# Start of a one-core decoder layer: order of the first loads, x turned by k-tile, two chunks interleaved

## The chip, the cores and the metric

The kernel runs on one core of a Trainium2 chip. The metric is the device time of one execution in microseconds; several executions are timed and their median is given. One further execution is profiled, and all rows of the trace below are from that one.

## What is computed

One layer of a decoder with parallel head groups, on 256 prompt tokens and 8 x 8 sample tokens (320 in all), all in float32:

```python
h = rmsnorm(x, g_mix_pre)                 # x: 320 tokens x 2048
p = h @ w_in                              # 2048 x 4352, columns: pool, conv (3 parts), u, v
ya = pool_mixer(p[pool], state_pool, pool_w, pool_scale)      # windows 2, 4, 8, 16
yb = short_conv_mixer(p[conv parts], state_conv, conv_w)
yc = sgu_mixer(p[u], p[v], sgu_norm, sgu_w, sgu_b)            # u * (tril(W) v + b)
x = x + rmsnorm(concat(ya, yb, yc) @ w_out, g_mix_post)
f = conv_ffn(rmsnorm(x, g_ffn_pre), state_ffn, ffn_up, ffn_conv_w, ffn_conv_b, ffn_down)
x = x + rmsnorm(f, g_ffn_post)            # and the new states
```

## The kernel before

Activations are held transposed: a k-tile is 128 features by 320 tokens, and the model width is 16 k-tiles. A product with a weight matrix is made one chunk of 128 output columns at a time. A chunk is 16 k-tiles, and for each k-tile three matmuls (`passes`, L474 to L485): high part by high part, high by low part of the weights, low part of the activations by high. Chunks go in pairs; chunk (q, e) is half e of pair q, accumulates in PSUM bank `mm[e]` and uses half e of `w_hi` and `w_lo`. The first six chunks, pairs 0 to 2, are the columns of u, the next six those of v.

Weights come from DRAM by SP's DMA queue (`load`, L374), 1 MB a chunk in runs of 512 bytes, into one of four places in `raw`. ScalarE copies them, rounded, into `w_hi` in two halves (`split_hi`, L813), and VectorE puts the rest into `w_lo` (`split_lo`, L1093). Counters order this: `landed[e]`, `w_hi_done`, `w_lo_done` (four counts a pair of each), `used` (a chunk's matmuls done) and `drained[e]`. SP's loads have no bound of their own but `w_hi_done`, and its DMAs are issued in program order.

At the start x comes in token order into `x_tok`, in four pieces of 512 columns, each by two DMAs (prompt, sample). TensorE turns it by transposes against an identity matrix (`turn_x`, L538), four k-tiles at a time and three token tiles each, into PSUM banks `tb[1]` to `tb[5]`; ScalarE and VectorE take turns in copying the results into `xT` (`copy_x`). ScalarE then scales and rounds each k-tile of `xT` into `a_hi` (L851), and VectorE makes `a_lo`, the rest (L1151). Chunk (0,0) is computed beside that, with its passes waiting for each k-tile.

After chunk (0,0) TensorE turns the small inputs (`small_inputs`, L562: gains, histories, the gating weights), for which it waits until all of them have landed; VectorE copies the results out of PSUM (L1156 to L1162, `hists_done`), then come chunk (0,1) and the pairs 1 and 2.

The norm's scale is not needed for u and v until late: GpSimd squares and sums the k-tiles of `xT` (`add_square`, L1581), the first eight as x arrives, then, after `hists_done`, a mask on the gating weights (L1598) and the other eight. TensorE reads the sum (`token_sums(0)`, L524) after the sixth chunk, behind a small matmul (`corners`, L589).

Of the kernel before, what the change touches and what calls it, by code (L numbers as in the profile page):

```python
# [31 lines left out]
def hybrid_layer(nc, x_prompt, x_sample, state_pool, state_conv, state_ffn, g_mix_pre, g_mix_post,  # L32
# [155 lines left out]

    with ExitStack() as ctx:
# [13 lines left out]
        x_in = [sem(f"x_in{i}") for i in range(KD // 4)]  # L203
# [87 lines left out]
        X_UNITS = 3 * (KD // 4)  # L291
# [3 lines left out]
        def x_units(k4, e):  # L295

            return [u for u in range(3 * k4, 3 * k4 + 3) if u % 2 == e] if k4 < KD // 4 else []

        def wait_x(engine, k4):

            for e in range(2):
                engine.wait_ge(x_copied[e], (3 * k4 + 4 - e) // 2)

        def x_unit(u):

            k4, i = u // 3, u % 3
            t0, nt = TT[i]
            return (xT[:, :].rearrange("p (k t) -> p k t", t=T)[:, 4 * k4:4 * k4 + 4, t0:t0 + nt],
                    tb[1 + u % 5][:, 0:4 * nt].rearrange("p (k t) -> p k t", k=4))
# [25 lines left out]
        def stage_vecs(q):  # L335
            rows = 0
            for v in (g_mix_pre, g_mix_post, g_ffn_pre, g_ffn_post, conv_w, sgu_norm, pool_scale):
                n = v.shape[-1] // P * (3 if v is conv_w else 1)
                src = v[0].rearrange("i (j c) -> (i j) c", c=P) if v is conv_w else \
# [26 lines left out]
        def _(sp):  # L366
# [20 lines left out]
            load(0, 0, wcols(win_v, U0))  # L387
# [13 lines left out]
            for e in range(2):  # L401
                load(1, e, wcols(win_v, U0 + 2 + e))
# [71 lines left out]
        def _(pe):  # L474
# [63 lines left out]
            def turn_x(k4):  # L538

                pe.wait_ge(x_in[k4], 32)  # L540
                for i in range(3):
                    u = 3 * k4 + i
                    if u >= 5:
                        pe.wait_ge(x_copied[(u - 5) % 2], (u - 5) // 2 + 1)
                    nt = TT[i][1]
                    for k in range(4):
                        b = 4 * k4 + k
                        last = pe.transpose(tb[1 + u % 5][:, k * nt:(k + 1) * nt],
                                            x_tok[0:nt, i, b * P:(b + 1) * P], ident[0:nt, 0:nt])
                    last.then_inc(x_turned, 1)  # L550


            pe.wait_ge(gain_in, 16)
            pe.transpose(tb[0][:, 0:KD], vec_raw[0:KD, 0, :], ident[0:KD, 0:KD]).then_inc(vecs_t, 1)
# [3 lines left out]
            turn_x(0)  # L558
            chunk(0, 0, a_hi, a_lo, order, lambda n: (a_hi_done, n + 1), lambda n: (a_lo_done, n + 1),
                  {n: [lambda k4=k4: turn_x(k4)] for k4, n in ((1, 0), (2, 1), (3, 5))})  # L560

            def small_inputs():  # L562
# [6 lines left out]
                for e in range(2):  # L569
                    pe.wait_ge(x_copied[e], X_UNITS // 2)  # L570
# [20 lines left out]

            small_inputs()
            chunk(0, 1, a_hi, a_lo, order, hurry=True)
# [1122 lines left out]
```

## Time and profile before

| | |
|---|---|
| median of 3 runs | 1370.25 us (1367.58 to 1371.25) |
| the profiled execution | 1367.87 us, its span 1366.1 us |
| TensorE busy | 1335.0 us, 98% |
| VectorE, ScalarE, GpSimd busy | 762.2, 504.9, 116.4 us |
| DMA over the span | 199.55 MB, 146 GB/s |
| mean granted TensorE clock | 0.993 |

The span is the time from the first to the last recorded instruction; about 1.8 us of the execution lie outside it. Busy time of TensorE counts overlapping pieces once; a matmul of 320 columns is recorded at 0.31 us, and the next one starts 0.15 us after it when nothing is waited for. The interval from one start to the next is what a matmul costs.

### The profile page before, as it was taken

What the parts mean: (1) busy time and instruction counts of PE and PEld (TensorE: products, weight loads), DVE (VectorE), ACT (ScalarE), POOL (GpSimd) and SP (SyncE); (2) the same over time, 40 slices, a digit from 0 to 9 for tenths busy, and PEclk for the clock granted to TensorE, in tenths of its full rate; (3) what the DMA queues carried; (4) which work ended last, traced back from release to release, by engine and by line L of the source; (5) the groups of instructions that cost most, each with busy time, mean ns of one, the idle gap of its engine ahead of it and who ended that gap; (6) DMA issues with size and microseconds to landing.
All of it is one profiled execution on the core that took longest, in us unless ns stands there. A gap on an engine that the chain in (4) does not pass through costs nothing.

```text
span 1366.1 us, 24821 instructions
## 1 busy us (share of the span) xinstructions
PE 1335.0 (98%) x9003; PEld 1319.6 (97%) x9003; DVE 762.2 (56%) x1170; ACT 504.9 (37%) x730; POOL 116.4 (9%) x225
## 2 busy tenths in 40 slices
PE   6999999999989999999999999999999999999997
PEld 5999999999978999999999999999999999999995
DVE  6447755553358655544555654455555445656445
ACT  4333422334345333333333333333333333333653
POOL 4542000000025000000000000000000000000001
PEclk9999999999989999999999999999999999999999
DMA  8555355555543555456555545655544565554453
GB/s 232 160 143 154 99 154 154 151 133 149 157 124 95 152 154 145 117 148 181 147 154 152 145 124 150 169 150 154 154 126 134 148 175 154 154 149 129 118 155 100
DMA packets 379007, 199.55 MB, mean 146 GB/s; under 512 B 3924, under 2 KB 374592, under 8 KB 378968
## 3 DMA queue, kind: packets, MB, share of 16 engines
q1 hardware_dynamic: 378896, 198.83, 53.0%
q8 instruction: 19, 0.31, 0.1%
q0 software_dynamic: 80, 0.31, 0.1%
q14 instruction: 12, 0.10, 0.0%
HBM read 195.68 MB, written 3.56 MB: 146 GB/s over the span
## 4 chain that ended last, share of the span: by engine, by line
PE 94%; DVE 2%; SPq 2%; POOL 1%; DMA 0%; issue 0%; ACT 0%; DVEq 0%; ACTq 0%
PE mm L481 30%; PE mm L485 30%; PE mm L482 30%; POOL xT L1652 1%; SPq L341 1%; PE tb L732 1%; DVE y_tok L1536 1%; DMA sgu_bias<-in_sgu_b_dram 0%; DVE sq L1375 0%; DVE w_lo L1102 0%; PE tb L524 0%; SPq L355 0%; PE tb L481 0%; PE tb L482 0%; PE tb L485 0%
## 5 line engine op out<-in xcount | busy, mean ns | idle before, releaser
L481 PE MATMUL mm<-a_hi,w_hi 128*128 128x320 f32 x1888 | 586.9, 311 | 0.0
L485 PE MATMUL mm<-a_lo,w_hi 128*128 128x320 f32 x1888 | 584.2, 309 | 1.8 <-DVE a_lo L1151 1.8
L482 PE MATMUL mm<-a_hi,w_lo 128*128 128x320 f32 x1888 | 583.7, 309 | 0.0
L824 ACT ACTIVATE w_hi<-raw 128x1024 fp32r (+3 forms) x396 | 364.9, 970 | 448.8 <-PE mm L485 435.5
L1102 DVE TENSOR_TENSOR w_lo<-raw,w_hi 128x1024 fp32r<-128x1024 f32 (+1 forms) x396 | 434.7, 1139 | 130.7 <-ACT w_hi L824 130.6
L485 PEld LDWEIGHTS mm<-a_lo,w_hi 128*128 128x128 f32 x1888 | 354.6, 188 | 2.7 <-DVE a_lo L1151 2.5
L481 PEld LDWEIGHTS mm<-a_hi,w_hi 128*128 128x128 f32 x1888 | 354.8, 188 | 1.2
L482 PEld LDWEIGHTS mm<-a_hi,w_lo 128*128 128x128 f32 x1888 | 354.9, 188 | 0.3
L485 PE MATMUL mm<-m_lo,w_hi 128*128 128x320 f32 x916 | 283.1, 309 | 0.0
L481 PE MATMUL mm<-h_hi,w_hi 128*128 128x320 f32 x660 | 205.7, 312 | 0.0
L482 PE MATMUL mm<-h_hi,w_lo 128*128 128x320 f32 x660 | 203.9, 309 | 0.0
L485 PEld LDWEIGHTS mm<-m_lo,w_hi 128*128 128x128 f32 x916 | 171.9, 188 | 0.0
L482 PEld LDWEIGHTS mm<-h_hi,w_lo 128*128 128x128 f32 x660 | 124.0, 188 | 0.0
L481 PEld LDWEIGHTS mm<-h_hi,w_hi 128*128 128x128 f32 x660 | 123.9, 188 | 0.0
L1435 DVE TENSOR_TENSOR f<-mm,f 128x320 f32 (+1 forms) x60 | 29.5, 492 | 130.7 <-PE mm L485 130.7
L970 ACT ACTIVATE h_hi<-val 128x320 f32 (+1 forms) x44 | 20.8, 472 | 191.7 <-DVE val L1422 191.7
L1666 POOL COPY ffn_tail_p<-zf 128x2 f32 x44 | 15.0, 340 | 804.4 <-DVE zf L1402 804.4
L481 PE MATMUL mm<-m_hi,w_hi 128*128 128x320 f32 x256 | 79.2, 309 | 0.0
L482 PE MATMUL mm<-m_hi,w_lo 128*128 128x320 f32 x256 | 79.1, 309 | 0.0
L1419 DVE TENSOR_TENSOR val<-mm,r_v 128x320 f32<-128x320 f32 x42 | 20.7, 492 | 84.1 <-PE mm L485 84.1
L1398 DVE COPY zf<-ffn_hist 128x16 f32 (+1 forms) x44 | 7.8, 176 | 96.1 <-PE mm L485 94.4
L482 PEld LDWEIGHTS mm<-m_hi,w_lo 128*128 128x128 f32 x256 | 48.1, 188 | 0.0
(241 smaller groups left out, 833.9 us busy)
## 6 DMA issues: line engine op xcount, KB each, us to landing
raw<-in_ffn_up_dram SPq DMA_DIRECT2D x88, 1024.0 KB, 5.7
raw<-in_ffn_down_dram SPq DMA_DIRECT2D x60, 704.0 KB, 4.8
raw<-in_w_in_dram SPq DMA_DIRECT2D x34, 1024.0 KB, 5.6
raw<-in_w_out_dram SPq DMA_DIRECT2D x16, 1024.0 KB, 6.0
x_tok<-in_x_prompt_dram SPq DMA_DIRECT2D x4, 512.0 KB, 7.5
raw<-in_ffn_down_dram SPq DMA_DIRECT2D x2, 1024.0 KB, 5.6
out_dram<-y_tok SPq DMA_DIRECT2D x8, 256.0 KB
raw<-in_ffn_down_dram SPq DMA_DIRECT2D x1, 768.0 KB, 4.3
```

Of the source, the lines that this page charges most:

```text
L341: yield q.dma_start(vec_raw[rows:rows + n, 0, :], src)
L481: pe.matmul(out, w_hi[:, s], hi, start=start, stop=False)
L482: pe.matmul(out, w_lo[:, s], hi, start=False, stop=False)
L485: return pe.matmul(out, w_hi[:, s], tile(lo, k), start=False, stop=stop)
L732: last = pe.transpose(bank[0:nt, k * P:(k + 1) * P], src[:, o:o + nt], ident[:, :])
L824: act.activation(w_hi[:, d:d + half], src, ACT.Copy).then_inc(w_hi_done, 1)
L970: act.activation(h_tile(i, 0, T), val[:, :], ACT.Copy).then_inc(h_hi_done, 1)
L1102: dve.tensor_tensor(w_lo[:, d], src, w_hi[:, d].bitcast(F32), ALU.subtract).then_inc(w_lo_done, 1)
L1419: dve.tensor_tensor(val[:, :], val_mm[:, 0:T], r_v[:, :], ALU.mult).then_inc(drained[1], 1)
L1435: dve.tensor_tensor(tile(f, m), mm[e][:, 0:T], tile(f, m), ALU.add).then_inc(drained[e], 1)
L1536: dve.scalar_tensor_tensor(out=piece, in0=f_tok[3 * k4 + i][0:nt, :], scalar=cols[0:nt, 2, i:i + 1], in1=piece, op0=ALU.mult, op1=ALU.add) ...
L1666: pool.tensor_copy(ffn_tail_p[:, bass.ds(n * CH, CH)], zf[:, LC - CH:LC])
```

## The change

- SP's first DMAs are in another order. x comes in five parts of 2, 2, 4, 4, 4 k-tiles. The weights of chunk (0,0) come in parts of 4, 4 and 8 k-tiles, those of (0,1) in two of 8, and they stand between the parts of x. The load of chunk (1,0) is issued after a wait on `w_hi_done`, and ahead of the small inputs; that of (1,1) after them. The first gain vector is issued from ScalarE's queue.
- x is turned one k-tile at a time, three transposes into one PSUM bank of six. ScalarE and VectorE make `a_hi` and `a_lo` straight from PSUM, and copy `xT` beside that, ScalarE the even and VectorE the odd k-tiles.
- Chunks (0,0) and (0,1) are interleaved: in step n come the turning of k-tile n + 2, the passes of k-tile n for chunk (0,0), and those of k-tile n - 10 for chunk (0,1).
- The weights of the two are split in the same parts, between the k-tiles: after k = 0, 4, 6, 11 and the last, on ScalarE into `w_hi` and on VectorE into `w_lo`.
- The small inputs are turned after chunk (1,0), and VectorE copies them after it has split the weights of chunk (1,1).
- GpSimd starts its squares when the weights of the first pair are all split and all of x is copied.

```diff
+    X_PARTS = [(0, 2), (2, 2), (4, 4), (8, 4), (12, 4)]
...
+            load_x(0)
+            load_part(0, 0, 4, w_in_part[0])
+            load_x(1)
+            load_x(2)
+            load_part(0, 4, 4, w_in_part[1])
+            load_part(0, 8, 8, landed[0])
+            load_x(3)
+            load_part(1, 0, 8, w_in_part[2])
+            load_x(4)
+            load_part(1, 8, 8, landed[1])
+            sp.wait_ge(w_hi_done, 2)
+            load(1, 0, wcols(win_v, U0 + 2))
             vecs = stage_vecs(sp)
-            next(vecs).then_inc(gain_in, 16)
-            for k4 in range(KD // 4):
-                cs = slice(k4 * 512, (k4 + 1) * 512)
-                sp.dma_start(x_tok[:, 0:2, cs], xp[:, :, cs]).then_inc(x_in[k4], 16)
-                sp.dma_start(x_tok[0:TS, 2, cs],
-                             x_sample.rearrange("b t d -> (b t) d")[:, cs]).then_inc(x_in[k4], 16)
-            load(0, 1, wcols(win_v, U0 + 1))
+            next(vecs)
             for d in vecs:
                 d.then_inc(vecs_in, 16)
             for d in stage(sp):
                 d.then_inc(staged, 16)
-            for e in range(2):
-                load(1, e, wcols(win_v, U0 + 2 + e))
+            sp.wait_ge(w_hi_done, 4)
+            load(1, 1, wcols(win_v, U0 + 3))
...
+            def turn_x(k):
+                n = X_PART[k]
+                if k == X_PARTS[n][0]:
+                    pe.wait_ge(x_in[n], 32)
+                if k >= 6:
+                    pe.wait_ge(*copied(k - 6))
+                for t0, nt in TT:
+                    last = pe.transpose(tb[k % 6][:, t0:t0 + nt], x_tok[0:nt, t0 // P, k * P:(k + 1) * P],
+                                        ident[0:nt, 0:nt])
+                last.then_inc(x_turned, 1)
...
+            AHEAD, LAG = 2, 10
+            for k in range(AHEAD):
+                turn_x(k)
+            pe.wait_ge(vecs_done, 1)
+            for n in range(KD + LAG):
+                k = n
+                if k < KD:
+                    if k + AHEAD < KD:
+                        turn_x(k + AHEAD)
+                    if k == 0:
+                        pe.wait_ge(first_lo, 1)
+                    if k in (4, 8):
+                        pe.wait_ge(w_lo_done, k // 4)
+                    last = passes(mm[0][:, 0:T], 0, k, a_hi, a_lo, k == 0, k == KD - 1,
+                                  (a_hi_done, k + 1), (a_lo_done, k + 1))
+                    if k == KD - 1:
+                        last.then_inc(used, 1)
+                k = n - LAG
+                if k >= 0:
+                    if k in (0, 8):
+                        pe.wait_ge(w_lo_done, 3 + k // 8)
+                    last = passes(mm[1][:, 0:T], 1, k, a_hi, a_lo, k == 0, k == KD - 1)
+                    if k == KD - 1:
+                        last.then_inc(used, 1)
...
+            chunk(1, 0, a_hi, a_lo, order)
             small_inputs()
-            chunk(0, 1, a_hi, a_lo, order, hurry=True)
-            with pe.Fori(1, NSGU // 2) as q:
+            chunk(1, 1, a_hi, a_lo, order)
+            with pe.Fori(2, NSGU // 2) as q:
                 pair(q, a_hi, a_lo, order)
...
+            act.dma_start(vec_raw[0:KD, 0, :], g_mix_pre[0].rearrange("(j c) -> j c", c=P)).then_inc(gain_in, 16)
...
             for k in range(KD):
-                if k % 4 == 1:
-                    copy_x(k // 4 + 1)
-                if k % 4 == 0:
-                    wait_x(act, k // 4)
-                act.activation(tile(a_hi, k), tile(xT, k), ACT.Copy,
+                act.wait_ge(x_turned, k + 1)
+                act.activation(tile(a_hi, k), tb[k % 6][:, 0:T], ACT.Copy,
                                scale=col(V_MIX_PRE + k)).then_inc(a_hi_done, 1)
-            split_hi(0, 1)
+                if k % 2:
+                    act.wait_ge(a_lo_done, k)
+                    act.activation(tile(xT, k - 1), tb[(k - 1) % 6][:, 0:T], ACT.Copy).then_inc(x_copied[0], 1)
+                if k == 0:
+                    split_part(0, 0, 4, w_in_part[0], first_hi)
+                if k == 4:
+                    split_part(0, 4, 4, w_in_part[1], w_hi_done)
+                if k == 6:
+                    split_part(0, 8, 8, landed[0], w_hi_done)
+                if k == 11:
+                    split_part(1, 0, 8, w_in_part[2], w_hi_done)
+            split_part(1, 8, 8, landed[1], w_hi_done)
...
                 dve.wait_ge(a_hi_done, k + 1)
-                dve.scalar_tensor_tensor(out=tile(a_lo, k), in0=tile(xT, k), scalar=col(V_MIX_PRE + k),
+                dve.scalar_tensor_tensor(out=tile(a_lo, k), in0=tb[k % 6][:, 0:T], scalar=col(V_MIX_PRE + k),
                                          in1=tile(a_hi, k).bitcast(F32), op0=ALU.mult,
                                          op1=ALU.subtract).then_inc(a_lo_done, 1)
-            split_lo(0, 1)
+                if k % 2:
+                    dve.tensor_copy(tile(xT, k), tb[k % 6][:, 0:T]).then_inc(x_copied[1], 1)
...
+            for e in range(2):
+                split_lo(1, e)
             dve.wait_ge(hists_t, 1)
...
-            for e in range(2):
-                split_lo(1, e)
...
+            pool.wait_ge(w_lo_done, 4)
+            for e in range(2):
+                pool.wait_ge(x_copied[e], KD // 2)
             for k in range(KD):
-                if k % 4 == 0:
-                    wait_x(pool, k // 4)
```

## Rows read from the trace of the kernel before

**Rows 1.** The page, engines: busy us (share of the span) xinstructions.
```profile
PE 1335.0 (98%) x9003; PEld 1319.6 (97%) x9003; DVE 762.2 (56%) x1170; ACT 504.9 (37%) x730; POOL 116.4 (9%) x225
```
**Rows 2.** The chain that ended last: shares, then one piece (start us, us).
```profile
PE 94%; DVE 2%; SPq 2%; POOL 1%; DMA 0%; issue 0%; ACT 0%; DVEq 0%; ACTq 0%
...
70.97 0.76 PE tb L524 x6
```
**Rows 3.** Timeline of PE (start us, us, what, count [idle before]), and a window with PEclk.
```profile
9.20 2.58 PE L548 MATMUL tb<-ident,x_tok 128*128 128x128 f32 x12 [1.70 <-DMA x_tok<-in_x_sample_dram]
...
15.39 0.47 PE L482 MATMUL mm<-a_hi,w_lo 128*128 128x320 f32 x1
15.65 0.47 PE L485 MATMUL mm<-a_lo,w_hi 128*128 128x320 f32 x1
...
20.41 1.42 PE L548 MATMUL tb<-ident,x_tok 128*128 128x128 f32 x12
...
31.68 0.63 PE L573 MATMUL tb<-ident,pool_raw 120*128 120x120 f32 x4 [1.82 <-DMA sgu_bias<-in_sgu_b_dram]
...
39.03 0.31 PE L482 MATMUL mm<-a_hi,w_lo 128*128 128x320 f32 x1
39.18 0.31 PE L485 MATMUL mm<-a_lo,w_hi 128*128 128x320 f32 x1
...
32.00:35.70 3.70, 3.70 (x19) 0.56 1.17 297
```
**Rows 4.** Timeline of ACT and DVE; then durations of two lines, min/median/max ns.
```profile
6.47 2.00 ACT L824 ACTIVATE w_hi<-raw 128x1024 fp32r<-128x1024 f32 x2 [4.38 <-DMA raw<-in_w_in_dram]
...
36.55 2.01 ACT L824 ACTIVATE w_hi<-raw 128x1024 fp32r<-128x1024 f32 x2 [6.46 <-DMA raw<-in_w_in_dram]
42.61 0.44 ACT L858 ACTIVATE f<-mm 128x320 f32<-128x320 f32 x1 [4.04 <-PE mm L485]
...
34.91 0.42 DVE L1156 COPY vec<-tb 128x252 f32<-128x252 f32 x1 [3.49 <-PE tb L582]
...
37.50 0.35 DVE L1162 COPY ffn_hist<-tb 128x192 f32<-128x192 f32 x1
37.76 3.02 DVE L1102 TENSOR_TENSOR w_lo<-raw,w_hi 128x1024 fp32r<-128x1024 f32 x2
...
L1151 DVE SCALAR_TENSOR_TENSOR a_lo<-xT,vec,a_hi x16: 535/1002/1160, 13.0 to 28.6; 128x320 fp32r<-128x320 f32 x16
...
L1220 DVE SCALAR_TENSOR_TENSOR m_lo<-tb,vec,m_hi x4: 546/550/551, 136.0 to 164.3; 128x320 fp32r<-128x320 f32 x4
```
**Rows 5.** Timeline of POOL: first square, eighth sum, mask, last sum.
```profile
12.29 0.72 POOL L1583 TENSOR_TENSOR acc<-xT 128x320 f32<-128x320 f32 x1 [8.41 <-ACT xT L842]
...
25.95 1.00 POOL L1586 TENSOR_TENSOR acc<-acc,sq 128x320 f32<-128x320 f32 x1
38.01 1.70 POOL L1598 TENSOR_SCALAR_AFFINE_SELECT ws<-ws 128x768 f32<-128x768 f32 x1 [11.06 <-DVE ffn_hist L1162]
...
57.29 0.88 POOL L1586 TENSOR_TENSOR acc<-acc,sq 128x320 f32<-128x320 f32 x1
```
**Rows 6.** Timeline of SP's queue; then landing times of the loads into raw.
```profile
8.41 0.61 SPq L385 DMA_DIRECT2D raw<-in_w_in_dram  x1
9.06 7.64 SPq L341 DMA_DIRECT2D vec_raw<-in_g_mix_post_dram  x1
...
26.58 4.85 SPq L385 DMA_DIRECT2D raw<-in_w_in_dram  x2
...
27.35 4.08 SPq L385 DMA_DIRECT2D raw<-in_w_in_dram  x1
...
DMA to landing us min/median/max: 5.6/8.1/12.2
```
**Rows 7.** Windows from the span's start: length, PEclk, DMA share, GB/s.
```profile
0.00:16.70 16.70, 1.00 0.93 249
0.00:31.43 31.43, 1.00 0.85 225
```

More of the change, by code:

```diff
@@ L187, in hybrid_layer @@
     ffn_out = sb("ffn_out", [P, 7, P], where="m_hi", plus=NG * HW * 4)
+    X_PARTS = [(0, 2), (2, 2), (4, 4), (8, 4), (12, 4)]
+    X_PART = [n for n, (k0, nk) in enumerate(X_PARTS) for _ in range(nk)]
     with ExitStack() as ctx:
@@ L202, in hybrid_layer @@
         drained = [sem(f"drained{i}") for i in range(2)]
-        x_in = [sem(f"x_in{i}") for i in range(KD // 4)]
+        x_in = [sem(f"x_in{i}") for i in range(len(X_PARTS))]
+        w_in_part = [sem(f"w_in_part{i}") for i in range(3)]
+        first_hi = sem("first_hi")
+        first_lo = sem("first_lo")
         gain_in = sem("gain_in")
@@ L289, in tile, with copied @@
             return t[:, k * T:(k + n) * T] if type(k) is int else t[:, bass.ds(k * T, n * T)]
-        X_UNITS = 3 * (KD // 4)
         MERGED = (4, 9)
         EARLY = 2
-        def x_units(k4, e):
-            return [u for u in range(3 * k4, 3 * k4 + 3) if u % 2 == e] if k4 < KD // 4 else []
-        def wait_x(engine, k4):
-            for e in range(2):
[L302 to L309, printed above, removed]
+        def copied(k):
+            return x_copied[k % 2], k // 2 + 1
         def h_tile(i, lo, hi):
@@ L338, in stage_vecs @@
                 n = v.shape[-1] // P * (3 if v is conv_w else 1)
+                if v is g_mix_pre:
+                    yield None
+                    rows += n
+                    continue
                 src = v[0].rearrange("i (j c) -> (i j) c", c=P) if v is conv_w else \
@@ L385, in load, with load_x, load_part @@
                 sp.dma_start(dst.rearrange("p (k c) -> p k c", c=width), src).then_inc(landed[e], 16)
-            load(0, 0, wcols(win_v, U0))
             xp = x_prompt[0].rearrange("(t p) d -> p t d", p=P)
-            vecs = stage_vecs(sp)
-            next(vecs).then_inc(gain_in, 16)
-            for k4 in range(KD // 4):
-                cs = slice(k4 * 512, (k4 + 1) * 512)
-                sp.dma_start(x_tok[:, 0:2, cs], xp[:, :, cs]).then_inc(x_in[k4], 16)
-                sp.dma_start(x_tok[0:TS, 2, cs],
-                             x_sample.rearrange("b t d -> (b t) d")[:, cs]).then_inc(x_in[k4], 16)
-            load(0, 1, wcols(win_v, U0 + 1))
+            def load_x(n):
+                k0, nk = X_PARTS[n]
+                cs = slice(k0 * P, (k0 + nk) * P)
+                sp.dma_start(x_tok[:, 0:2, cs], xp[:, :, cs]).then_inc(x_in[n], 16)
+                sp.dma_start(x_tok[0:TS, 2, cs],
+                             x_sample.rearrange("b t d -> (b t) d")[:, cs]).then_inc(x_in[n], 16)
+            def load_part(e, k0, nk, sem):
+                o = (e * KD + k0) * P
+                sp.dma_start(raw[:, o:o + nk * P].rearrange("p (k c) -> p k c", c=P),
+                             wcols(win_v, U0 + e)[:, k0:k0 + nk]).then_inc(sem, 16)
+            load_x(0)
[10 more added lines that the diff above has]
+            load(1, 0, wcols(win_v, U0 + 2))
+            vecs = stage_vecs(sp)
+            next(vecs)
             for d in vecs:
@@ L536, in _ @@
             pe.wait_ge(consts, 1)
[L538 to L550, printed above, removed]
@@ L553, in _ @@
-            pe.wait_ge(gain_in, 16)
-            pe.transpose(tb[0][:, 0:KD], vec_raw[0:KD, 0, :], ident[0:KD, 0:KD]).then_inc(vecs_t, 1)
-            order = range(KD)
-            turn_x(0)
-            chunk(0, 0, a_hi, a_lo, order, lambda n: (a_hi_done, n + 1), lambda n: (a_lo_done, n + 1),
-                  {n: [lambda k4=k4: turn_x(k4)] for k4, n in ((1, 0), (2, 1), (3, 5))})
+            def turn_x(k):
[8 more added lines that the diff above has]
+                last.then_inc(x_turned, 1)
@@ new lines, in _ @@
+            order = range(KD)
+            pe.wait_ge(gain_in, 16)
+            pe.transpose(mm[1][:, 0:KD], vec_raw[0:KD, 0, :], ident[0:KD, 0:KD]).then_inc(vecs_t, 1)
+            AHEAD, LAG = 2, 10
[22 more added lines that the diff above has]
+                        last.then_inc(used, 1)
```

40 lines of the change are left out of this document (20 added, 20 removed).

## The prediction

> **What bounds the kernel now.** I read the page's engine table first: TensorE is busy 98% of the span, the next engine, VectorE, 56% [rows 1]. The chain that ended last puts 94% on TensorE and 2% on the SP queue [rows 2], so the only place where loads cost time is the start. From about 36 us on TensorE runs one matmul after the other: starts 0.15 us apart (39.03 to 39.18), 48 of them to a chunk, 7.05 us a chunk, with ScalarE draining the second chunk at 42.61 [rows 3, 4]. Two chunks are 14.1 us of that work, so 28.5 us of the first 42.6 are something else. The reader is to see four things in the timeline there: TensorE starts turning x only at 9.20, behind 1 MB of weights; early matmuls start 0.26 us apart (15.39, 15.65), which is the 1.2 GHz level, against 0.15 at 2.4 GHz; it waits 1.82 us for the last small input at 31.68; and it is granted only 0.56 of its clock from 32 to 35.7 [rows 3, 6]. After that nothing stops it until the sum of squares is read at 70.97 [rows 2], and I take that matmul as the landmark: all behind it is unchanged and follows on it, so what it moves by is what the kernel moves by. It needs two chains: TensorE's own six chunks, and GpSimd's squares, which now end at 58.2, 12.8 us early [rows 5].
>
> **Loads.** The x pieces and the first weights are cut and mixed; the sum is the same until both first chunks are in, 2.62 MB of x and 2.10 MB of weights. Before, 1.05 MB had landed at 6.47 (ScalarE's wait) and the second block, 4.73 MB in, at 20.6 (8.41 plus the longest landing, 12.2) [rows 4, 6]. That is 0.26 MB per us. The new last x part ends at 4.19 MB, so it lands at 6.47 + 3.14/0.26 = 18.5, the first x part (0.33 MB) at about 4 (two microseconds after issue, an estimate; x at 4 or at 6 changes nothing below). x begins earlier and does not end earlier. The gain vector goes to ScalarE's queue and is off the path: it is wanted at 4, and even the 5.6 us of the shortest landing in the list [rows 6] would delay only k-tiles that wait for x afterwards. SP's two new waits, on the second and fourth high weight part, hold every later load behind them; the parts land at 11.5 and 20.5 by the same rate and are split 1 to 5 us later, before SP is free again at 16.7 and 30.2, as worked out below, so they cost nothing. ScalarE's wait for the part of chunk (0,1), landing at 16.0, holds up k-tile 12, which is not there before 18.5.
>
> **First two chunks.** TensorE is in order and turns k-tile 12 before the passes of k-tile 10, so it cannot go beyond k-tile 9 before 18.5, whatever VectorE does. Behind that lie 12 transposes at 0.12 (1.42 us for 12 [rows 3]) and 6 + 16 passes of 3 matmuls, 66 x 0.147 = 9.7: 11.1 us, end 29.6. TensorE has waited for x shortly before, so I add low clock: 3.7 us at 0.56 [rows 3] cost some 1.6, and all 66 at 0.26 would cost 7.5. I take 1.5: both chunks end at 31, between 29.6 and 38. VectorE and ScalarE are not the bound here: 16 splits at 0.55 (a split read from PSUM took 0.55, and one beside GpSimd's squares up to 1.16 [rows 4]), 8 copies at 0.5 and 3.5 us of weight splits are 16.3 us from about 5.5; even at 1.0 a split the last four need less than TensorE's 1.23 us a k-tile. Copies of xT lie beside that. The Trainium skill ("TensorE: Matmul & The Clock Gate", Part 1) says that throttled is the default state and activity releases it; the trace agrees (0.26 us apart at the start, 0.15 later). By that rule the waits for x keep the clock low, which by the rows above would put the end at 31.2 and not 29.6; it speaks for the late side.
>
> **Third chunk and small inputs.** Chunk (1,0) is 7.05: 38. Its weights wait until chunk 0 releases the buffers 4.8 us before chunk 1 ends; drain 0.4, first half by ScalarE 1.0, two halves by VectorE 2.4 to 3.0 make 3.8 to 4.4, so nothing is lost. The small inputs are 20 transposes; the last 17 took 3.2 us at mostly low clock before, 31.68 to VectorE's start at 34.91 [rows 3, 4], and 20 at 0.12 are 2.4 at the high one, which I take: TensorE is ready for chunk (1,1) at 40.5. The 1.8 us wait for them is gone.
>
> **The fourth chunk's load.** This is the term that decides. SP's issues are held back when too much is outstanding: the first small input was issued at 9.06 and went through after 7.64, at 16.7, when 249 GB/s x 16.7 = 4.16 of 4.84 MB had moved, 0.68 MB left; the load issued at 27.35 went through at 31.43, when 7.07 of 7.72 MB had moved, 0.64 left [rows 6, 7]. Now load (1,0), 1.05 MB, stands ahead of the small inputs, and at the full-queue rate of 0.27 MB per us they begin 4.0 us later, 20.7 for 16.7. SP then issues the same 19 DMAs, one each 0.5 us, and load (1,1) at 26.58 + 4.0 = 30.6. The load that stood in that place, with another behind it as now, was first touched at 36.55, 10.0 us after its issue [rows 4, 6]. So load (1,1) lands at 40.5. ScalarE takes 1.05 for the first half, VectorE 2.35 to 3.02 for both (3.02 beside GpSimd): chunk (1,1) can start at 44.3, and TensorE waits 3.8 us. Counting bytes alone, all up to that load were through at 33.5 before, so the slowest of the rings cost the rest; if that is not repeated it lands at 37.5 to 38.5. Both ends are kept.
>
> **Squares.** GpSimd now starts when the fourth part of the low weights is there, about 27, and its first eight squares took 14.7 (12.29 to 26.95) [rows 5]: 42 to 45 with the weight splits beside. The second eight wait for the small inputs' copies. These stand behind the split of chunk (1,1) on VectorE, 44.3, and took 2.94 (34.91 to 37.85): 47.2. From 37.85 to the end of the squares at 58.2 was 20.3 with the mask in it [rows 4, 5]: 67.5. TensorE's own chain: 44.3 + 7.05 + 1.6 to 2.0 of low clock after the wait + 14.1 = 67.1 to 67.5. Both meet at 67.5, and the 12.8 us of slack of the squares is used up. Weights of later chunks are a chunk ahead and come through.
>
> **Sum.** The landmark goes from 71.0 to 67.5: 3.5 us less. The profiled execution took 1367.87 (span 1366.1 and 1.8 around it), so 1364.4 by its own time. That is 2.4 below the median of the runs, 1370.25, so 1366.8 in those terms. A difference of 0.3%, 4.1 us, is what a measurement can tell from none.
>
> **Rivals.**
> A, the forecast: the fourth chunk's load decides, gain 2.6 to 4.6. Chance 0.50.
> B: the load comes by bytes, at 38.5 or before. For it: landings are 5.6 us when the queue is short, against it the 10.0 of the same place. Chunk (1,1) can start at 42.1, copies end at 45.0, squares at 65.3: gain 5.7. With the load no bound at all the small inputs are, at 40.5: squares at 63.7, then low clock 1.6 after TensorE's wait of 2 us, 65.3, gain 5.7. So the squares cap what a quicker start may bring. About 1364.5, chance 0.22.
> C: the small inputs come 1 to 3 us later still, or the first two chunks end at 35 to 37 (three separate waits for x at low clock), or GpSimd's first eight run into the second. Gain 0.5 to 2.6, about 1368.7, chance 0.22.
> D, the other side: the clock stays at the 1.2 GHz level through the first chunks, as each new wait (k-tiles 4, 8, 12) comes before it rises. 66 matmuls at 0.26 and 12 transposes at 0.21 from 18.5 end at 38.2; small inputs end at 48.8, squares at 72.0: 1 us slower. Low clock in chunk (1,0) too, 48 at 0.26 for 7.05, makes it 77.5, 6.5 us slower, 1376.8. It turns to a loss when the two chunks end after 37. Against it: 2.4 GHz was reached by 19 before, in spite of the 1.70 us wait, and a TensorE at the low clock is late enough to have few waits left. Chance 0.06.
>
> **Numbers.** Faster by over 0.3%: all but a little of B and the upper quarter of A, 0.20 + 0.14 and 0.03 for scatter: 0.37. Slower by over 0.3%: most of D, 0.04. Within: 0.59. The range goes from B less a microsecond (1363.0) to C's far end (1370.0), which leaves out D and the tails; A's own is 1365.6 to 1367.7.
>
> **What would show it.** Right: the last x transposes after 18; TensorE idle for 3 to 4 us before chunk (1,1) with the low weights as releaser; SP's first small input going through near 20.7; the first token sum at 67 to 68 with the squares ending just there; splits of x at 0.55. Wrong, if load (1,1) lands before 38, if TensorE does not wait before chunk (1,1), or if it waits for GpSimd by more than 2 us; if the landmark moves and the total does not, the step that all behind it follows fails.

## The result and the profile after

| | before | changed |
|---|---|---|
| median of 20 runs | 1370.22 us (1367.49 to 1371.69) | 1371.46 us (1369.13 to 1378.31) |
| ratio to before | | 1.0025, 95% interval 1.0016 to 1.0034 |
| profiled execution, span | 1367.87, 1366.1 us | 1373.18, 1371.4 us |
| first token sum starts (timeline of TensorE) | 70.90 us | 74.65 us |

The change makes the kernel slower by a quarter of a per cent. The forecast was 1366.8, faster by 3.5 us. The medians are 1.2 us apart and the means, 1369.8 and 1373.0, 3.2, because the changed kernel scatters: 11 of the 20 executions of the changed kernel lie between 1369.1 and 1371.8, 7 between 1374.0 and 1378.3, while those of before keep within 4.2 us. So what it lost differs from one execution to the next, and the profiled one, at 1373.18, is none of the 11: all rows of the changed kernel below tell how that one execution lost its 5.3 us of span.

I look first for the landmark, the first token sum. [rows 2] put it at 70.97 by the chain; by the timeline, which I use from here on for every run, it starts at 70.90 in the kernel before:

```profile
70.90 0.83 PE L524 MATMUL tb<-ones,acc 128*128 128x1 f32 x6
```

Timeline of TensorE in the changed kernel (start, length, instruction, what it waited for):

```profile
5.21 1.90 PE L561 MATMUL tb<-ident,x_tok 128*128 128x128 f32 x6 [2.02 <-DMA x_tok<-in_x_sample_dram]
7.32 0.96 PE L561 MATMUL tb<-ident,x_tok 128*128 128x128 f32 x3 [0.21 <-DMA x_tok<-in_x_sample_dram]
...
10.99 0.93 PE L561 MATMUL tb<-ident,x_tok 128*128 128x128 f32 x3
11.85 0.63 PE L496 MATMUL mm<-a_hi,w_hi 128*128 128x320 f32 x1
12.28 0.47 PE L497 MATMUL mm<-a_hi,w_lo 128*128 128x320 f32 x1
12.55 0.47 PE L500 MATMUL mm<-a_lo,w_hi 128*128 128x320 f32 x1
12.81 0.93 PE L561 MATMUL tb<-ident,x_tok 128*128 128x128 f32 x3
...
25.55 0.93 PE L561 MATMUL tb<-ident,x_tok 128*128 128x128 f32 x3
...
34.93 0.31 PE L497 MATMUL mm<-a_hi,w_lo 128*128 128x320 f32 x1
35.07 0.31 PE L500 MATMUL mm<-a_lo,w_hi 128*128 128x320 f32 x1
...
48.85 0.40 PE L599 MATMUL tb<-ident,vec_raw 92*128 92x92 f32 x3
...
51.09 0.41 PE L496 MATMUL mm<-a_hi,w_hi 128*128 128x320 f32 x1
...
74.65 0.92 PE L539 MATMUL tb<-ones,acc 128*128 128x1 f32 x6 [1.94 <-POOL acc L1631]
```

TensorE has x four microseconds sooner than in [rows 3] (5.21 against 9.20), and but for 0.21 us at 7.32 it does not wait for x again. One k-tile's turning and one k-tile's passes go round in 1.82 us, 10.99 to 12.81, and again 14.63, 16.45 and so on to 25.55. In that round the three transposes take 0.86 us, the first matmul behind them 0.43, and then matmuls start 0.27 us apart, which is the 1.2 GHz level; 0.15 us, the 2.4 GHz level, is seen from 34.7 on. The last line is the landmark, and it waits for GpSimd.

Windows of the changed kernel (length, PE busy, PEclk, DMA share, GB/s):

```profile
5.00:34.00 29.00, 28.35 (x93) 1.00 0.93 239
70.00:75.00 5.00, 3.06 (x22) 1.00 0.52 137
75.00:80.00 5.00, 5.00 (x26) 0.66 0.81 211
```

TensorE is busy in 28.35 of the 29 us from 5 to 34 and yet at half its speed. The clock column shows 1.00 there, but the trace holds no record of the clock before 34.3 us, so a first rise has to be read from the distance of two starts. From 75 to 80, behind the wait for GpSimd, the column does show a fall to 0.66; before, this stretch was at the full clock.

Timeline of the changed kernel on ScalarE, VectorE, GpSimd and the SP queue, in the same columns (for SP the second number is how long the issue took, or a run of alike issues from the first to the last):

```profile
42.01 0.44 ACT L898 ACTIVATE f<-mm 128x320 f32<-128x320 f32 x1 [2.51 <-PE mm L500]
42.40 2.01 ACT L858 ACTIVATE w_hi<-raw 128x1024 fp32r<-128x1024 f32 x2
...
53.79 0.35 DVE L1209 COPY ffn_hist<-tb 128x192 f32<-128x192 f32 x1
...
37.93 0.72 POOL L1628 TENSOR_TENSOR acc<-xT 128x320 f32<-128x320 f32 x1 [34.05 <-DVE w_lo L1182]
...
53.59 0.88 POOL L1631 TENSOR_TENSOR acc<-acc,sq 128x320 f32<-128x320 f32 x1
54.54 1.73 POOL L1644 TENSOR_SCALAR_AFFINE_SELECT ws<-ws 128x768 f32<-128x768 f32 x1
...
73.74 0.86 POOL L1631 TENSOR_TENSOR acc<-acc,sq 128x320 f32<-128x320 f32 x1
...
17.52 4.29 SPq L338 DMA_DIRECT2D vec_raw<-in_g_mix_post_dram  x1
...
31.14 0.55 SPq L354 DMA_DIRECT2D sgu_bias<-in_sgu_b_dram  x1
36.61 50.84 SPq L382 DMA_DIRECT2D raw<-in_w_in_dram  x8
```

The view of one line in the changed kernel, VectorE's low parts of x: least, median and longest duration in ns, first start and last end in us, and what VectorE waited for ahead of them (us, times):

```profile
L1186 DVE SCALAR_TENSOR_TENSOR a_lo<-tb,vec,a_hi x16: 544/550/552, 6.9 to 35.3; 128x320 fp32r<-128x320 f32 x16
its engine sat idle before it (us, times) until:
  ACT a_hi L880: 16.3, 12
```

Both first chunks are done at 42.0, as late as the second one was before (42.6 in [rows 4]), though the small inputs are not among them any more. VectorE makes each low part in 0.55 us and sits idle for 16.3 us between them, so it isn't the pace. The copies of the small inputs end at 54.14 (before 37.85), GpSimd's squares at 74.6, 20.5 after that, and TensorE, which would have been there at 72.7, waits 1.94 us. The landmark is 3.75 us late (1.8 of TensorE's own work and 1.94 of waiting), and the low clock behind it makes up the rest of the 5.3 us of the span.

### The profile page after: what moved, and what is told of

Its sections match the earlier page's. It is cut to its first block, busy times and chain, and to the rows that moved or that the text cites. A ratio compares the mean times of both kernels' runs of the same rounds, so it can differ in the third digit from the quotient of the medians.

```text
span 1371.4 us, 24821 instructions
## 1 busy us (share of the span) xinstructions
PE 1346.2 (98%) x9003; PEld 1325.6 (97%) x9003; DVE 760.3 (55%) x1173; ACT 505.4 (37%) x733; POOL 118.2 (9%) x225
## 4 chain that ended last, share of the span: by engine, by line
PE 92%; POOL 4%; DVE 2%; issue 0%; ACT 0%; DMA 0%; SPq 0%; DVEq 0%; ACTq 0%
PE mm L496 30%; PE mm L497 29%; PE mm L500 29%; POOL xT L1698 1%; POOL acc L1631 1%; POOL sq L1628 1%; PE tb L561 1%; PE tb L765 1%; DVE y_tok L1581 0%; DMA x_tok<-in_x_sample_dram 0%; DVE sq L1420 0%; DVE w_lo L1142 0%; PE tb L539 0%; PE tb L496 0%; PE tb L497 0%
## 5 line engine op out<-in xcount | busy, mean ns | idle before, releaser
L858 ACT ACTIVATE w_hi<-raw 128x1024 fp32r (+3 forms) x392 | 360.9, 969 | 437.7 <-PE mm L500 435.3
L1464 DVE TENSOR_TENSOR val<-mm,r_v 128x320 f32<-128x320 f32 x42 | 20.7, 492 | 84.1 <-PE mm L500 84.1
L496 PEld LDWEIGHTS mm<-m_hi,w_hi 128*128 128x128 f32 x256 | 48.1, 188 | 0.0
```

Of the source, the lines that this page charges most:

```text
L496: pe.matmul(out, w_hi[:, s], hi, start=start, stop=False)
L858: act.activation(w_hi[:, d:d + half], src, ACT.Copy).then_inc(w_hi_done, 1)
L1464: dve.tensor_tensor(val[:, :], val_mm[:, 0:T], r_v[:, :], ALU.mult).then_inc(drained[1], 1)
```

## The experiments

Rows one to four, five to eight and nine to twelve of the table share a chip each, and the ratio is to the executions of the kernel before on that chip (medians 1369.87, 1369.30 and 1369.70). Each run has 11 or 12 executions, the last two have five. "Both end" is where ScalarE starts to drain the second chunk; the wait in the last column is for GpSimd's squares.

| run | median us | ratio, 95% interval | both end | first token sum, its wait |
|---|---|---|---|---|
| squares early | 1370.94 | 1.0007, 0.9995 to 1.0018 | 41.96 | 74.32, 1.66 |
| and mask last | 1371.70 | 1.0013, 1.0003 to 1.0023 | 39.57 | 70.69, none |
| no interleave | 1372.86 | 1.0022, 1.0011 to 1.0032 | 41.98 | 74.35, 1.67 |
| 14 extra matmuls | 1369.65 | 0.9993, 0.9980 to 1.0005 | 36.94 | 69.55, 1.91 |
| 14 extra, squares early, mask last | 1367.03 | 0.9983, 0.9974 to 0.9992 | 37.89 | 68.52, none |
| bursts of four | 1368.04 | 0.9991, 0.9979 to 1.0002 | 34.49 | 67.83, 1.63 |
| 6 extra, no interleave, squares early, mask last | 1370.48 | 0.9999, 0.9982 to 1.0017 | 42.38 | 73.00, none |
| kernel before with 14 extra | 1366.97 | 0.9983, 0.9973 to 0.9993 | 40.49 | 68.79, none |
| bursts by token tile | 1366.19 | 0.9983, 0.9973 to 0.9993 | 32.01 | 67.60, 1.61 |
| that, 14 extra, squares early, mask last | 1366.66 | 0.9980, 0.9971 to 0.9989 | 33.57 | 66.52, none |
| that, load (1,1) earlier | 1362.40 | 0.9952, 0.9939 to 0.9966 | 32.28 | 63.39, none |
| the same without extra matmuls | 1361.73 | 0.9947, 0.9934 to 0.9961 | 34.53 | 65.53, none |

The last two columns are of one profiled execution each, which need not be near the median.

**Squares early.** One part undone:

```diff
-            pool.wait_ge(w_lo_done, 4)
-            for e in range(2):
-                pool.wait_ge(x_copied[e], KD // 2)
             for k in range(KD):
+                pool.wait_ge(*copied(k))
                 if k == KD // 2:
```

> The changed kernel with one part undone: GpSimd squares each k-tile as soon as it is copied, as before; the mask still stands in the middle. Theory 1 (the start is paced by TensorE at the 1.2 GHz level; GpSimd's second half is what the first token sum waits for, and it starts at the copies of the small inputs at 54.1): first half done by 45, second half from 54.2, first token sum at 74.3 instead of 74.65, total within 1 us of the changed kernel. Theory 2 (holding the squares back until the weights are split is the loss): token sum at 72.7, total 3.5 us less. The low parts of x read one PSUM and one SBUF operand: if GpSimd's squares slow them they take up to 1.0 us instead of 0.55.

The token sum moved by 0.33 us, as theory 1 had it: GpSimd's mask starts at 54.24, 0.3 earlier than with the squares late. Holding back the squares cost those 0.3 us in this trace, since the first half ran 0.3 past the copies; the rest of the wait comes from what the second half hangs on. The median is half a microsecond below the changed kernel's, measured on another chip, and that can't be told from nothing.

**Mask last.** The wait for the small inputs' copies out of the squares:

```diff
-                if k == KD // 2:
-                    pool.wait_ge(hists_done, 1)
-                    pool.affine_select(out=ws[:, :, :], in_=ws[:, :, :], compare_op=ALU.is_ge, fill=0.0,
-                                       base=0, pattern=[[0, NSGU], [1, P]],
-                                       channel_multiplier=-1).then_inc(tril_done, 1)
                 add_square(tile(xT, k), k == 0, k == KD - 1)
+            pool.wait_ge(hists_done, 1)
+            pool.affine_select(out=ws[:, :, :], in_=ws[:, :, :], compare_op=ALU.is_ge, fill=0.0,
+                               base=0, pattern=[[0, NSGU], [1, P]],
+                               channel_multiplier=-1).then_inc(tril_done, 1)
```

> As the run before, and the mask on the gating weights after all sixteen squares instead of between eighth and ninth. Theory 1: nothing of the squares waits for the small inputs any more, they end before 56; TensorE reaches the first token sum at 72.7 and does not wait, and the low clock behind that wait (0.66 in 75 to 80) is gone: 1.9 and 1.6, together 3.5 us less than the changed kernel, about level with the kernel before. Theory 2 gives nothing beyond the run before.

The wait at the token sum is gone, and so is the low clock behind it; the profiled execution took 1369.16, 3.6 less than the one with the squares early. But the median did not fall (1371.70, against 1370.94 for the squares early on the same chip), and the trace shows why one execution says little here: in this one the clock rose at 21 and fell again after a wait. Timeline of TensorE with the mask last:

```profile
20.14 0.47 PE L500 MATMUL mm<-a_lo,w_hi 128*128 128x320 f32 x1
20.40 0.93 PE L561 MATMUL tb<-ident,x_tok 128*128 128x128 f32 x3
21.26 0.41 PE L496 MATMUL mm<-a_hi,w_hi 128*128 128x320 f32 x1
21.51 0.30 PE L497 MATMUL mm<-a_hi,w_lo 128*128 128x320 f32 x1
21.65 0.31 PE L500 MATMUL mm<-a_lo,w_hi 128*128 128x320 f32 x1
...
26.68 0.42 PE L496 MATMUL mm<-a_hi,w_hi 128*128 128x320 f32 x1 [1.54 <-DVE w_lo L1182]
```

The same instructions that stayed at 0.27 us until 34 in the changed kernel's trace are at 0.15 from 21 here, at 0.27 again from 28 to 31. So the cut into single k-tiles does not forbid the high clock; it leaves open when it comes. The expected 3.5 us of median was a miss, and no run shows what the wait at the token sum costs in the median.

**No interleave.**

```diff
-            AHEAD, LAG = 2, 10
+            AHEAD, LAG = 2, 16
```

> The changed kernel without the interleave: chunk (0,1) follows chunk (0,0), 16 k-tiles behind instead of 10. Theory 1, with the transposes as what keeps the clock low: four steps of 0.8 us at the low clock move behind the last transpose and run at 0.147 a matmul; both chunks end 1.1 to 1.5 us earlier than 42.0. If the second chunk's matmuls are what raises the clock, it rises later and both end at 42 to 44. A theory in which x's landing paces the start gives no change before k-tile 10 and an end later by none.

A miss of the 1.1 to 1.5 us: both end at 41.98. The low-clock steps of 1.82 us go on to 33.4, and the clock rises at 34.3, where it did with the interleave. In this trace the second chunk's passes among the first's neither cost nor gain.

**Fourteen extra matmuls.** Float32 matmuls of 128 columns whose results nobody reads, before the first x is turned, to have the clock up:

```diff
             AHEAD, LAG = 2, 10
+            for _ in range(14):
+                pe.matmul(tb[5][:, 0:P], ones[:, :], ident[:, :], start=True, stop=True)
```

> The changed kernel with 14 extra float32 matmuls of 128 columns, whose results nobody reads, on TensorE before the first x k-tile is turned (about 3.2 to 8.5 us, so x is turned some 3 us later than it could be). Theory 1: the clock is at 2.4 GHz from about 7.5 on and the start holds it; steps of a k-tile go from 1.82 to 0.9 us until TensorE waits for x; both chunks end at 30 to 33 instead of 42.0, and then the terms of the prediction that were never reached decide: chunk (1,1) waits for its load until 44, token sum at 67 to 69. Rival (work cut this fine does not hold the clock): it falls back to matmuls 0.26 apart, both chunks end at 43 to 45. Rival (loads of x pace the start): both chunks end at 42 or later in spite of a high clock.

Timeline of TensorE with 14 extra matmuls (a float32 matmul of this kind is recorded as two, hence x28):

```profile
3.20 5.75 PE L571 MATMUL tb<-ident,ones 128*128 128x128 f32 x28
8.79 1.73 PE L561 MATMUL tb<-ident,x_tok 128*128 128x128 f32 x9
11.31 0.41 PE L496 MATMUL mm<-a_hi,w_hi 128*128 128x320 f32 x1 [0.79 <-DVE w_lo L1184]
...
12.92 0.58 PE L561 MATMUL tb<-ident,x_tok 128*128 128x128 f32 x3
...
13.98 0.58 PE L561 MATMUL tb<-ident,x_tok 128*128 128x128 f32 x3
...
24.07 0.42 PE L496 MATMUL mm<-a_hi,w_hi 128*128 128x320 f32 x1 [1.45 <-DVE w_lo L1184]
```

The round of a k-tile falls from 1.82 to 1.06 us and stays there until 22, so the loads of x were not the pace, and the finely cut work holds a high clock that it has. Both end at 36.94, five microseconds earlier though x is turned 3.6 later; the 30 to 33 expected did not come, because of that start, the 1.45 us wait at k-tile 10 and a fall of the clock behind it (25.1 to 28.6). The load of chunk (1,1) was first touched at 40.20, waited for by ScalarE alone. GpSimd still holds the token sum for 1.91 us.

**Both losses taken away.** The two losses are the low clock of the first chunks and the wait at the token sum. The edits of "squares early", "mask last" and "fourteen extra matmuls" together (these unread matmuls are added work in every run that has them):

> The run with 14 extra float32 matmuls (results unread) and the run with the mask after all squares, together. Theory (low clock through the first chunks, and GpSimd's squares behind the small inputs' copies, are the two losses and add up): TensorE reaches the first token sum at 67.3 as in the run with extra matmuls alone, does not wait there (1.9 there), and the low clock of 70 to 77 behind it is gone: median 1366 to 1367, some 3.5 below the run with extra matmuls alone (1369.65). Rival (the low clock behind the wait has nothing to do with it, or the load of chunk (1,1) takes over): 1369 or more.

1367.03, 2.6 below the extra matmuls alone, but on another chip; by the ratios, 0.9983 and 0.9993, it is 1.4, and their intervals overlap. From 68 to 77 the clock is full, where it was 0.57 from 69 to 77 in the run with extra matmuls alone. So both losses are gone from the trace (token sum at 68.52, expected 67.3), and that they add up in the median is not shown.

**Bursts of four.** x turned four k-tiles at a time, all else as changed:

```diff
-                    if k + AHEAD < KD:
-                        turn_x(k + AHEAD)
+                    for t in {0: (2, 3), 2: (4, 5, 6, 7), 6: (8, 9, 10, 11), 10: (12, 13, 14, 15)}.get(k, ()):
+                        turn_x(t)
```

> The changed kernel with x turned in bursts of four k-tiles (12 transposes, as before), all else as changed. Theory A (turning by single k-tiles costs TensorE time by itself: three transposes and the change to matmuls take 0.86 us at the low clock, 12 in a row 2.5): 0.9 us less for four k-tiles, both chunks end near 38.7 even if the clock does not rise earlier. Theory B (and it is the fine cut that keeps the clock low): in the kernel before, with bursts, it rose near 18.8; here too it is up by 20, k-tile steps go to about 1 us, and both chunks end at 32 to 35. If neither, they end at 41 to 42.

Timeline of TensorE with bursts of four:

```profile
10.89 3.67 PE L561 MATMUL tb<-ident,x_tok 128*128 128x128 f32 x12
14.48 0.63 PE L496 MATMUL mm<-a_hi,w_hi 128*128 128x320 f32 x1
...
22.28 2.31 PE L561 MATMUL tb<-ident,x_tok 128*128 128x128 f32 x12
24.52 0.41 PE L496 MATMUL mm<-a_hi,w_hi 128*128 128x320 f32 x1
```

ScalarE in the same trace:

```profile
34.49 0.44 ACT L898 ACTIVATE f<-mm 128x320 f32<-128x320 f32 x1 [2.51 <-PE mm L500]
40.52 2.01 ACT L858 ACTIVATE w_hi<-raw 128x1024 fp32r<-128x1024 f32 x2 [5.58 <-DMA raw<-in_w_in_dram]
```

Theory B, and not A: 12 transposes take 3.6 us at the low clock (10.89 to 14.48), four times 0.90, so a burst in itself saves nothing on the transposes. But the clock is up by 20.4 and both end at 34.49. One edit of the order on TensorE takes back 7.5 of the first 42 us, and 3.4 us of median against the changed kernel (on another chip; the intervals of the two ratios, to 1.0002 and from 1.0016, do not meet). Now the load of chunk (1,1) holds ScalarE from 34.9 to 40.52.

**Six extra matmuls, no interleave, mask last.** The edits of "both losses taken away" (squares early too), with two numbers changed:

```diff
-            AHEAD, LAG = 2, 10
-            for _ in range(14):
+            AHEAD, LAG = 2, 16
+            for _ in range(6):
```

> A version made from the findings: 6 extra matmuls instead of 14 (so that x is not held back), the second chunk after the first, squares early and the mask last. Theory (a start at the high clock is what counts): k-tile steps of 1.06 us from about 8.5, or from 10 if six are too few to raise it; both chunks end at 32.5 to 34.5, first token sum at 63 to 65.5 unless the load of chunk (1,1) takes over, which landed at 40.2 in the run with 14: then at 67. Median 1364 to 1368. Rival: six are too few, the clock stays low as in the changed kernel, both chunks end at 41 to 42.

In the profiled execution six were too few: 1.82 us a round, both end at 42.38, the rival's case. The 12 executions fall in two clumps, five from 1363.1 to 1366.1 and six from 1372.1 to 1373.4, 7 us apart. The one profiled is of the upper clump and started at the low clock; that the lower ones started at the high clock is likely, but no trace of one is kept. The expected 1364 to 1368 was a miss.

**The kernel before with the extra matmuls.** Nothing of the change is in it:

```diff
+            for _ in range(14):
+                pe.matmul(tb[5][:, 0:P], ones[:, :], ident[:, :], start=True, stop=True)
             pe.wait_ge(gain_in, 16)
```

> The kernel before with the same 14 extra matmuls, where TensorE waits for the first vector and x in any case. Theory (the start of the kernel before is bound by the landing of the small inputs at 31.68, not by TensorE): the clock is high from the first k-tile on and chunk (0,0) may end earlier, but the small inputs are turned at the same time; only the low clock of 32 to 35.7 might change; landmark at 69.5 to 71, median within 1.5 us of the kernel before. Rival (TensorE's low clock bounds that start too): chunk (0,0) and all behind it 2 to 4 us earlier.

Part of it was wrong. The small inputs are turned at 31.10, 0.6 earlier, so their landing does bound that start; but the stretch from 32 to 35.7, at 0.56 in [rows 3], is now at the full clock. Window of that run (length, PE busy, PEclk, DMA share, GB/s):

```profile
32.00:35.70 3.70, 3.70 (x28) 1.00 1.20 290
```

The landmark is at 68.79, 2.1 earlier, and the median 2.3 lower. I had called the start of before not bound by TensorE; the 0.6 us and some 1.6 of low clock were its own. On this one chip two runs can be compared: the kernel before with 14 extra matmuls takes 1366.97, and the changed kernel with them and both fixes of the squares 1367.03. With the clock high from the start in both, the change gains nothing.

**Bursts by token tile.** Inside a burst, the four tiles of tokens 0 to 127 first, then the next four, then the four of 64 samples:

```diff
...
+                for t0, nt in TT:
+                    for k in ks:
+                        ins = pe.transpose(tb[k % 6][:, t0:t0 + nt],
+                                           x_tok[0:nt, t0 // P, k * P:(k + 1) * P], ident[0:nt, 0:nt])
+                        if t0 == TT[-1][0]:
+                            ins.then_inc(x_turned, 1)
...
```

> The changed kernel, x turned in bursts of four k-tiles and inside a burst by token tile (four of 128 tokens, four of 128, four of 64) instead of 128, 128, 64 for each k-tile. Theory (going from a 128-row tile to a 64-row one and back costs by itself; 12 transposes took 3.6 at the low clock in the run with bursts and 2.5 in the kernel before): 12 take 2.5 at the low clock and 1.45 at the high one, both chunks end 2 to 4 us before the 34.5 of that run, unless x's landing takes over. The first token sum does not move below 67, since the load of chunk (1,1) lands at 40 and GpSimd's second half hangs on the small inputs: median 1367 to 1368.5. Rival: 12 still take 3.6; nothing changes.

Timeline of TensorE in that run:

```profile
15.77 1.48 PE L574 MATMUL tb<-ident,x_tok 128*128 128x128 f32 x12 [0.26 <-DMA x_tok<-in_x_sample_dram]
19.93 1.48 PE L574 MATMUL tb<-ident,x_tok 128*128 128x128 f32 x12 [0.73 <-DMA x_tok<-in_x_sample_dram]
...
44.36 0.41 PE L496 MATMUL mm<-a_hi,w_hi 128*128 128x320 f32 x1 [3.21 <-DVE w_lo L1156]
```

ScalarE and the SP queue in the same trace: the load of chunk (1,1) is first touched at 40.86 and was issued at 32.15, the first of nine alike:

```profile
40.86 2.00 ACT L872 ACTIVATE w_hi<-raw 128x1024 fp32r<-128x1024 f32 x2 [8.41 <-DMA raw<-in_w_in_dram]
32.15 52.95 SPq L382 DMA_DIRECT2D raw<-in_w_in_dram  x9
```

12 transposes take 1.48 us for 2.31, with the same clock and the same work, so going between 128-row and 64-row tiles costs by itself. Which PSUM bank they write is not the reason: sorted transposes take 1.42 with four in a row in one bank ([rows 3]) and 1.48 with each in another. Both end at 32.01, and x's landing is now felt: the last part is there at 19.93, after a wait of 0.73. TensorE waits 3.21 us for chunk (1,1), which starts at 44.36; the prediction had 3.8 and 44.3. With 1366.19 it is below the expected 1367 to 1368.5. In this trace the clock was up by 12.6, where it took the bursts of four until 18 to 20; in the last run below, with the same sorted bursts, matmuls start 0.27 apart until 17.7, so the sorting alone does not bring it.

**With extra matmuls, squares early and mask last; then the load moved.** The first of these two runs is the bursts by token tile and the edits of "both losses taken away" together. The second is the first with load (1,1) in front of the small inputs. The last weight part of the first pair gets a semaphore of its own, so that this load need not wait on the fourth high part:

```diff
...
             load(1, 0, wcols(win_v, U0 + 2))
+            load(1, 1, wcols(win_v, U0 + 3))
             vecs = stage_vecs(sp)
...
-            sp.wait_ge(w_hi_done, 4)
-            load(1, 1, wcols(win_v, U0 + 3))
...
```

> That, with the 14 extra matmuls, squares early and the mask last. Theory: the first chunks end at 31 to 33, TensorE waits 2 to 4 us before chunk (1,1) for its load (landed at 40.2 to 40.7 in three runs, split until 44), as the prediction had it; first token sum at 66 to 67, no wait there; median 1365 to 1366.5. Rival (the load is no bound): first token sum at 63 to 64, 1363.

> The run before this one with the load of chunk (1,1) issued ahead of the small inputs instead of behind them. Theory (that load's place in the queue is the next bound): it lands before 30, small inputs land near 39.5, where TensorE wants them; chunk (1,1) starts at 41 to 43 instead of 44 to 45; first token sum at 62.5 to 64.5; 1362 to 1364.5. Rival (small inputs now come later and hold TensorE as much): they land after 43, no gain.

Against the bursts by token tile alone (1366.19, same chip) the first of the two gains nothing, 1366.66, though its wait at the token sum is gone: the extra matmuls hold back x, both end at 33.57 instead of 32.01, and the load of chunk (1,1) is touched at 41.46. Then the load moves: token sum from 66.52 to 63.39, median from 1366.66 to 1362.40. Its place in the queue is worth 4 us once the first chunks are quick. In the second trace TensorE waits 0.3 us for the small inputs at 39.78 and not at all for chunk (1,1).

**Without the extra matmuls.** The run with the load moved, without its 14 unread matmuls:

> The same without the 14 extra matmuls. Theory: x is turned from 5.3 instead of 9, the clock rises near 18 to 20 by itself; both chunks end at 31 to 34, first token sum at 63 to 66; 1363 to 1366. Rival (without the extra matmuls the clock stays low in most executions): both end at 38 to 42, median 1369 or more.

1361.73, ratio 0.9947, below the expected 1363 to 1366: the lowest median of the study, some 7 us below the kernel before (0.0053 of 1369.7), though it can't be told from the run with the extra matmuls (0.9952; the intervals overlap). Five executions, 1361.4 to 1365.6; the profiled one is the slowest of them. With bursts by token tile the extra matmuls are not needed.

## Why the prediction was wrong

**The step that failed** is "first two chunks": both at 31, "between 29.6 and 38". They ended at 42.0. I let TensorE stand at k-tile 9 until x's last part landed at 18.5, and priced only what lies behind it: 12 transposes at 0.12 and 66 matmuls at 0.147, 1.5 us added for the clock. TensorE reached that place at 25.55, 7 us after I had x landed, because the ten rounds before it cost 1.82 us each, a price I never worked out because I had them hidden behind x's landing. From there to the end of both it took another 16.5 us, where I had 11.1 and 1.5 for the clock.

Three terms make the 1.82. The clock: the extra matmuls bring it to 1.06 with nothing else changed. The order of the transposes: 0.86 for three, where the rows that I took the price from [rows 3] are sorted by tile shape; sorted, 12 cost 1.48, unsorted 2.31 at the same clock. And the change from transposes to matmuls: the first matmul behind them costs 0.43 for 0.27 (0.25 for 0.15 at the high clock), once in every round of the fine cut and once in four k-tiles with bursts.

The first term was rival D, to which I gave 0.06 and an end at 38.2. D was right about the clock and wrong about its reason, since it wanted new waits for x. My argument against it, that a TensorE at the low clock has few waits left, was true (0.23 us of waits from 8 to 34) and no argument: the clock stayed low without waits. One of the signs that I had named for being wrong came: TensorE does not wait before chunk (1,1).

**Where the forecast does come true** is the run with bursts by token tile: x's last part at 19.93 (18.5), both chunks at 32.01 (31), chunk (1,1) at 44.36 after 3.21 of waiting (44.3, 3.8), token sum at 67.60 (67.5), median 1366.19 (1366.8; the kernel before is at 1369.70 on that chip). With the order of the transposes that I had priced, the sum was sound; part of that is luck, as the load below shows, and there TensorE waits 1.61 for GpSimd, where I had none.

**When the clock rose.** That activity releases the throttle (the Trainium skill, "TensorE: Matmul & The Clock Gate", Part 1) I weighed only through waits. The traces agree that the clock comes up with work, and they show TensorE busy in 28.35 of 29 us at the low level. It was up by 20.4 with the same transposes in bursts, and at 21 in one execution without. In the other four traces of the fine cut that did not start high it rose at 34.0 to 35.4, with the last transposes of x or behind them. What about a burst raises it, no run here isolates.

**The squares** were right as a chain. Second half ending 20.3 us after the copies (measured 20.5), all slack used up, TensorE waiting: 1.94 us. I had both chains meet without a wait; the low clock behind the wait, priced under B at 1.6, came too. As a start I gave 27, and it was 37.93, again by the first step; the first half then ran until 54.47, 0.3 past the end of the copies at 54.14, so that any later end of it would have cost in full.

**The fourth chunk's load**, which I named as the term that decides, did not in the changed kernel: ScalarE splits it at 42.40, right behind the drain of the second chunk at 42.01, and waits for no load. As a time it was right in the runs with a quicker start: it was touched at 40.20, 40.66, 40.52, 40.86 and 41.46 (predicted 40.5), and the wait for it showed as up to 3.21 us. That is in part luck. I had it issued at 30.6 and touched 10.0 later; in those runs it was issued at 32.0 to 32.5 and touched 8.2 to 9.3 later. The first small input went through at 21.8 (predicted 20.7). One premise failed in the changed kernel itself: SP's wait on the fourth high part, said to cost nothing, held the load until 36.61, since ScalarE splits that part only after the last k-tile.

**Third chunk and small inputs** took 7.04 us (41.81 to 48.85) and 2.24 (48.85 to 51.09), where I had 7.05 and 2.4. **VectorE's price** was 0.55 for each low part, as taken.

**Where the gain went.** Work was to be moved into a stretch where TensorE stood idle. TensorE filled that stretch, but at half the speed, so that the two chunks were done at 42.0 in place of 42.6; the small inputs, 2.2 us, which had been inside the 42.6, came on top. Turned and copied behind chunk (1,0), they start GpSimd's second half 16.3 us later, and it had 12.8 us to spare. That is the account of the profiled execution; the 11 that took 1369 to 1372 lost less, and no trace of one is kept.

## What to carry to other kernels

Where work is moved into an idle stretch at the start, price it at the low clock first, on the engine that does it, and look at what its order does to the cost of one piece: sort transposes by tile shape, which needs bursts of several k-tiles. A chain with slack (here the squares, 12.8 us) has that slack only as long as the thing that releases its second half stays where it is: follow the wait inside it, not its first start. A bound that is right in size decides only after those before it are gone; take them away one by one, and it returns.

## What the runs showed of the hardware

- The granted clock in the windows read 1.00 from the start, while matmuls of 320 columns started 0.27 us apart until 34 us. The trace has no record of the clock before 34.3 (18.7 in the kernel before), so the first rise is seen in the starts only, and the 1.00 of [rows 7] and the mean of 0.993 say nothing of that stretch.
- The same program can spread over 9 to 10 us (1369.1 to 1378.3 the changed kernel, 1363.1 to 1373.4 the one with 6 extra matmuls, in two clumps). The clock came up at 21 in one trace of the fine cut and at 34 to 35 in four, which fits, but the executions of the clumps were not traced one by one. Single executions, the profiled one too, can't be compared to a microsecond there.
- Twelve transposes in the order 128, 128, 64 rows took 3.6 us at the low clock and 2.3 at the high one; sorted by shape 2.5 to 2.6 and 1.4 to 1.5.
- The first matmul of 320 columns behind transposes was followed by the next after 0.43 us at the low clock and 0.25 at the high one, where in a row of matmuls it is 0.27 and 0.15.
- VectorE's low parts of x, which took up to 1.16 us beside GpSimd's squares before [rows 4], took 0.55 beside them when one operand was in PSUM (median 549 ns, squares early). Line of that run: durations min/median/max.

```profile
L1186 DVE SCALAR_TENSOR_TENSOR a_lo<-tb,vec,a_hi x16: 537/549/551, 7.0 to 35.3; 128x320 fp32r<-128x320 f32 x16
```

The Trainium skill ("GPSIMD Engine Reference", Specifications) says that GpSimd's SBUF interfaces contend with VectorE's instructions that have two SBUF inputs; both rows agree. So, as far as VectorE goes, the squares could have stayed early.
